# The order of scores, transposed probabilities and turns in the attention stage of a hybrid decoder step

## What is computed

```
qkv, z, b_lg, a_lg, qb, kb, vb, ga, gb = in_proj(hp, norm1_w[l], w_in[l])
q, k, v, g, beta, conv_new = delta_prep(qkv, zeros, b_lg, a_lg, ...)   # causal conv (4 taps) + SiLU, 12 x 128 channels
o_a, s_new = gated_delta_chunked(q, k, v, g, beta, zeros)
y_a = delta_out(o_a, z, delta_norm_w[l], w_proj_a[l])
y_b = moba_prompt(rope(qb), rope(kb), vb) @ w_proj_b[l]                # causal softmax attention, 8 heads of 64
hp = merge_and_mlp(hp, y_a, y_b, ga, gb, w_out[l], ...)                # then squared-ReLU MLP
```

## Time and profile before

| | us |
|---|---|
| three runs | 1039.46, 1040.54, 1044.44 (median 1040.54) |
| the profiled execution | 1039.46 |
| its span in the trace | 1037.3 |
| TensorE busy | 982.2 (95%) |
| VectorE busy | 540.4 (52%) |
| ScalarE busy | 398.5 (38%) |
| GpSimd busy | 235.2 (23%) |

### The profile page before, as it was taken

The page is one execution under the profiler, slowest core; times in us unless marked ns, Lnnn a source line. Parts: engine busy times, 40 slices in busy tenths (PEclk is TensorE's granted clock), DMA queues, the critical chain, the costliest instruction groups (busy, mean ns, idle before and its releaser), DMA issues.

```text
span 1037.3 us, 20446 instructions
## 1 busy us (share of the span) xinstructions
PE 982.2 (95%) x7854; PEld 927.0 (89%) x7854; DVE 540.4 (52%) x727; ACT 398.5 (38%) x673; POOL 235.2 (23%) x137
## 2 busy tenths in 40 slices
PE   5999799999898898999999999998999999999997
PEld 5999788899898676777789999998999999999996
DVE  5246599898678534313314755784344334334443
ACT  6435445555513235332222333342154235224433
POOL 0017666567646301100000000493000000000000
PEclk9999899999978899999999999999999999999998
DMA  8576676667665246777864384235333333233312
GB/s 249 161 239 199 206 227 185 201 176 211 187 179 149 61 127 201 211 211 206 245 176 138 114 263 135 83 102 153 102 92 91 93 91 92 89 93 89 93 41 82
DMA packets 182313, 156.75 MB, mean 151 GB/s; under 512 B 9153, under 2 KB 144011, under 8 KB 181846
## 3 DMA queue, kind: packets, MB, share of 16 engines
q1 hardware_dynamic: 167382, 143.75, 47.2%
q10 hardware_dynamic: 14856, 11.97, 3.6%
HBM read 146.84 MB, written 8.95 MB: 150 GB/s over the span
## 4 chain that ended last, share of the span: by engine, by line
PE 74%; DVE 8%; issue 6%; ACT 4%; POOL 4%; SPq 2%; DMA 1%; ACTq 0%; DVEq 0%; POOLq 0%
PE ps L457 58%; PE ps L2037 5%; PE ps L2028 3%; POOL ring L752 3%; ACT w_high L441 2%; DVE uu L1679 1%; PE ps L1893 1%; DVE w_low L446 1%; SPq L579 1%; DVE lg L1213 1%; DMA ring<-in_cache_v 1%; PE ps L2044 1%; PE ps L1711 1%; SPq L580 1%; PE ps L1860 1%
## 5 line engine op out<-in xcount | busy, mean ns | idle before, releaser
L457 PE MATMUL ps<-xh,w_high 128*128 128x256 f32 x1216 | 258.8, 294 | 7.1 <-DVE cvr L1258 4.3
L446 DVE TENSOR_TENSOR w_low<-w_raw,w_high 128x1024 fp32r<-128x1024 f32 x125 | 165.7, 1325 | 162.8 <-ACT w_high L441 162.3
L457 PE MATMUL ps<-xl,w_high 128*128 128x256 f32 x1216 | 247.3, 285 | 0.0
L457 PE MATMUL ps<-xh,w_low 128*128 128x256 f32 x1216 | 247.0, 285 | 0.0
L441 ACT ACTIVATE w_high<-w_raw 128x1024 fp32r<-128x1024 f32 x125 | 132.2, 1057 | 258.2 <-PE ps L457 255.4
L457 PEld LDWEIGHTS ps<-xh,w_high 128*128 128x128 f32 x1216 | 190.3, 191 | 22.2 <-issue 19.5
L457 PEld LDWEIGHTS ps<-xl,w_high 128*128 128x128 f32 x1216 | 191.2, 191 | 0.0
L457 PEld LDWEIGHTS ps<-xh,w_low 128*128 128x128 f32 x1216 | 190.9, 190 | 0.0
L752 POOL TENSOR_TENSOR ring<-ring,qb 128x1024 f32<-128x1024 f32 x64 | 153.3, 2419 | 140.8 <-DVE mtqk L1228 73.2
L457 PE MATMUL ps<-mh,w_high 128*128 128x256 f32 (+1 forms) x640 | 128.6, 282 | 3.4 <-DVE ml L1669 3.4
L457 PE MATMUL ps<-mh,w_low 128*128 128x256 f32 (+1 forms) x640 | 128.9, 283 | 0.0
(11 more groups left out here) (358 smaller groups left out, 1243.3 us busy)
## 6 DMA issues: line engine op xcount, KB each, us to landing
ring<-in_cache_k SPq DMA_DIRECT2D x128, 256.0 KB, 3.0
ring<-in_cache_v SPq DMA_DIRECT2D x128, 256.0 KB, 3.0
w_raw<-in_w_in SPq DMA_DIRECT2D x66, 256.0 KB, 3.9
w_raw<-in_w_up SPq DMA_DIRECT2D x64, 256.0 KB, 3.0
w_raw<-in_w_down SPq DMA_DIRECT2D x64, 256.0 KB, 3.0
w_raw<-in_w_in ACTq DMA_DIRECT2D x24, 256.0 KB, 4.1
w_raw<-in_w_out SPq DMA_DIRECT2D x16, 256.0 KB, 3.4
ht_dram<-ht ACTq DMA_DIRECT2D x1, 2080.0 KB, 14.1
```

The costliest lines, as they stand in the source:

```text
L446: dve.tensor_tensor(w_low[:, u % 2], w_raw[:, u % 4], w_high[:, u % 2].bitcast(F32), ALU.subtract).then_inc(S_lo, 1)
L457: last = pe.matmul(out[:, a:b], w[:, u % 2, k, :], x[:, i, a:b], start=(first + i == 0 and w is w_high and x is rhs_h), stop=(first + i == ...
```

## The change

It changes the order in which three engines issue the operations of a step, and with it which score is computed in which step.

- PE, step n: before, on odd n two scores (n + 1 and n + 2) in a row, a quarter, `turn_probs(n)`, `pv_prompt(n − 1)`, a quarter, then `turn_conv` and `turn_rows_out`. After, `turn_probs(n)`, the score n + 2 by itself, a quarter, `pv_prompt(n − 1)`, `turn_rows_out`, `turn_conv`, a quarter.
- ACT, step n: before, taps (or tanh), `exp_scores(n + 1)`, `turned_probs(n)`, `conv_turned_out`, `split_high`. After, `turned_probs(n)`, `exp_scores(n + 1)`, taps, `conv_turned_out`, `split_high` on odd n, tanh on even n.
- DVE: `maxima(n + 2)` in step n in place of `maxima(n + 1)`.
- The table of constants gets two more blocks of 128 columns, which nothing reads.

```diff
-K_ID, K_ONE, K_TRI, K_CAUS, K_LT8, K_ROPE = 0, 128, 256, 384, 512, 576
+K_ID, K_ONE, K_TRI, K_CAUS, K_STRICT, K_INCT, K_LT8, K_ROPE = 0, 128, 256, 384, 512, 640, 768, 832
...
             for n in range(NA):
                 q_t, h = divmod(n, HB)
                 m = (n - 1) // 2
+                turned_probs(n)
+                if n + 1 < NA:
+                    exp_scores(n + 1)
                 if n % 2:
                     if m < NC12:
                         conv_taps(m)
                     else:
                         z_tanh(m)
-                elif 2 <= n <= 2 * NC12:
-                    conv_tanh((n - 2) // 2)
-                if n + 1 < NA:
-                    exp_scores(n + 1)
-                turned_probs(n)
-                if n % 2:
                     if 1 <= m <= NC12:
                         conv_turned_out(m - 1)
                     split_high(act, U_C + m + 2)
+                elif 2 <= n <= 2 * NC12:
+                    conv_tanh((n - 2) // 2)
...
+            maxima(1)
             for n in range(NA):
                 q_t, h = divmod(n, HB)
                 m = (n - 1) // 2
-                if n + 1 < NA:
-                    maxima(n + 1)
+                if n + 2 < NA:
+                    maxima(n + 2)
...
             def scores(n):
                 q_t, h = divmod(n, HB)
                 r, N = slice(64 * (h % 2), 64 * (h % 2) + 64), (q_t + 1) * P
+                if n >= 2:
+                    pe.wait_ge(S["att_exp"], n - 1)
+                if n < 2:
+                    pe.wait_ge(S["mt_out"], 11 + n)
+                if n < HB:
+                    pe.wait_ge(S["qk_out"], 5 + n // 2)
                 mm(score_bank(n, N), qt[r, h // 2, q_t * P:(q_t + 1) * P], kt[r, h // 2, 0:N], start=True, stop=True)\
                     .then_inc(S["att_sums"], 1)
-
-            def score_pair(n):
-
-                pe.wait_ge(S["att_exp"], n)
-                if n < HB:
-                    pe.wait_ge(S["qk_out"], 5 + n // 2)
-                scores(n)
-                scores(n + 1)
...
             for n in range(NA):
-                if n % 2 and n + 1 < NA:
-                    score_pair(n + 1)
+                turn_probs(n)
+                if n + 2 < NA:
+                    scores(n + 2)
                 if n + 1 < 2 * NWOVEN:
                     quarter_unit(2 * n + 2)
-                turn_probs(n)
                 if n >= 1:
                     pv_prompt(n - 1)
+                if n % HB == TURN_AT and n >= HB:
+                    turn_rows_out(n // HB - 1)
+                if n % 2 and 3 <= n <= 2 * NC12 + 1:
+                    turn_conv((n - 3) // 2)
                 if n == NA - 1:
                     sum_new_rows()
                 if n + 1 < 2 * NWOVEN:
                     quarter_unit(2 * n + 3)
-                if n % 2 and 3 <= n <= 2 * NC12 + 1:
-                    turn_conv((n - 3) // 2)
-                if n % HB == TURN_AT and n >= HB:
-                    turn_rows_out(n // HB - 1)
```

More of the change, by code:

```diff
@@ L165, in constants @@
     c[:, K_CAUS:K_CAUS + P] = np.where(i[None, :] <= i[:, None], 0.0, -BIG)
+    c[:, K_STRICT:K_STRICT + P] = np.where(i[None, :] < i[:, None], 0.0, -BIG)
+    c[:, K_INCT:K_INCT + P] = np.where(i[:, None] <= i[None, :], 0.0, -BIG)
     n = np.arange(8)
@@ L1910, in _ @@
             quarter_unit(1)
-            pe.wait_ge(S["mt_out"], 11)
-            pe.wait_ge(S["qk_out"], 5)
             scores(0)
@@ L1915, in _ @@
             turn_moba_heads(7)
-            pe.wait_ge(S["mt_out"], 12)
             scores(1)
             for n in range(NA):
-                if n % 2 and n + 1 < NA:
-                    score_pair(n + 1)
+                turn_probs(n)
+                if n + 2 < NA:
+                    scores(n + 2)
                 if n + 1 < 2 * NWOVEN:
                     quarter_unit(2 * n + 2)
-                turn_probs(n)
                 if n >= 1:
                     pv_prompt(n - 1)
+                if n % HB == TURN_AT and n >= HB:
+                    turn_rows_out(n // HB - 1)
+                if n % 2 and 3 <= n <= 2 * NC12 + 1:
+                    turn_conv((n - 3) // 2)
                 if n == NA - 1:
```

## The result

| | before | after |
|---|---|---|
| median (us) | 1041.12 (4 runs) | 1054.46 (4 runs) |
| ratio, 95% interval | | 1.0125, 1.0105 to 1.0144 |
| median of a second set | 1041.18 (23 runs) | 1054.00 (6 runs) |
| ratio of that set | | 1.0120, 1.0102 to 1.0139 |
| profiled execution | 1039.46 | 1052.68 |

The changed kernel is slower by 1.2%, about 13 us. Forecast were a sum of +7.4 us, a time of 1047.5 and a range up to 1053.5: the direction was right, the size too small, and the median lies just outside the range.

A forecast was written before the change was run, and what follows sets the result against it. PE, busy for 95% of the span, was taken as the bound. From the profiled execution, 1039.46 + 11.5 − 4.3 + 1.7 − 1.5 = 1046.9 us, named as 1047.5; the forecast's own range was 1044.5 to 1052.5, the wider one 1042.5 to 1053.5.

The forecast's parts named there:

- The mechanism: PE, attention stage: a pair's heads run side by side, so each score left alone adds a slot; 11.5 us in all.
- the silu's stalls: PE's seven waits for conv_silu before first quarters, 4.3 us, go; new stalls of 1.7 us come, some 1.2 at n = 5.
- DVE's wait for `w_high`: DVE in the attention stage: its 7.1 us wait for w_high was to be gone with the earlier turn_conv.
- the wait for `gate_a`: PE at the end of the stage: the 1.87 us wait hangs on a chain of the same length and stays.
- The walk through the end of the stage: Chain from w_low of step 30 to att_n: att_n starts 7 us later, PE's own work arrives 8.5 later.
- wait for `att_n`: PE at turn_rows_out(3): the 1.48 us wait is absorbed, taken as −1.5 us in the sum.
- 15 slots: Attention stage: 15 single scores each hold PE for a pair's time, 0.43 to 1.06 us, adding 11.5 us.
- the entry of 0.09 us: A single score starts 0.09 us later than the spacing of records before it; paid 15 more times, only in a bound.
- my bound of 12.8: Upper bound on the added PE time of the slots, 12.8 us, with the late start of each single score.
- Faster: Rival: an added slot costs next to nothing and the stalls go, 1033.7 to 1035.4 us; chance 0.06.
- no change: Rival: PE takes the added time out of slack, 1039 to 1043 us; chance 0.14.
- Slower still: Rival: ACT's late taps stall DVE and PE in every pair, 12 times 0.5 us on top, 1053 us; chance 0.10.

The follow-up runs named there:

- experiment 4: Kernel before, pairs kept in a row, but every score reads partitions 0 to 63 of qt and kt: 1046.11 us, ratio 1.0041.
- experiment 2: Kernel before with the second score of each pair moved behind the quarter of a unit that followed the pair: 1054.30 us, ratio 1.0120.
- experiment 7: Changed kernel with ACT's old order, single scores kept: 1052.49 us, ratio 1.0098.
- 11: Kernel before with earlier turns, turn_probs right behind the pair on odd steps, and DVE's silu ahead of the reduces on even steps: 1036.88 us, ratio 0.9959.
- 6: Kernel before with ACT's new order alone: 1069.67 us, ratio 1.0272.
- experiment 1: Changed kernel with the scores in pairs again and maxima(n + 1) in step n, the other moves kept: 1056.38 us, ratio 1.0123.

## Why the prediction came out as it did

**The mechanism was right.** A score alone takes PE as long as a pair, at all widths (0.41 and 1.05 us), because the heads of a pair lie in different partitions (experiment 4). The waits moved as forecast: the silu's stalls went to two, the longest behind the convolution of n = 5 (0.8 us, forecast 1.2), DVE's wait for `w_high` went, one of `conv` for the taps came (1.4 us), the wait for `gate_a` stayed at 1.9. The walk through the end of the stage had its start wrong, though. The chain from `w_low` to `att_n` keeps its 10.3 us, but it starts at 270.28, 11.3 us later than before and not 7, and `gate_a` comes 11.3 later as well. PE arrives 12.3 later and not 8.5. That most of the wait for `att_n` was absorbed all the same came from two errors of like size.

**The step that failed is a term that was sized too small**: "so 15 slots are added: 3 of 0.43, 4 of 0.64, 4 of 0.85, 4 of 1.06, that is 1.3 + 10.2 = 11.5 us". I took the pair's time on PE as the price of a slot, and put the entry of 0.09 us in a bound only. By stretches without a stall a slot costs 1.19 to 1.23 us at 512 keys and 1.00 at 384, which is 0.13 to 0.17 above the values I took, and over all widths it is 0.15 above them (experiment 2). That is 11.5 + 15 · 0.15 = 13.7 us, which also lies above my bound of 12.8. The rise of PE's busy time in the stage, 14.1 us, agrees, where I had named 10. The 0.09 stood in the earlier trace rows. The rest is paid by the instruction behind the score, and the trace of before shows such a cost too: behind a pair the quarter's first two records take 0.35 us from start to start (243.39 to 243.74) where the next two take 0.23. I measured the pair up to the start of the next instruction and not through it.

**The waits, term by term.** The silu: −4.3 + 1.1 against my −4.3 + 1.7. `att_n`: 1.48 down to 0.45, so −1.0 against −1.5. Missed altogether: `turn_probs` at the head of a step waits for `attention_low`, +1.1. The sum as forecast and as the runs give it:

| term | forecast | measured |
|---|---|---|
| 15 slots | +11.5 | +13.7 (14 of them measured) |
| stalls for the silu, old and new | −2.6 | −3.2 |
| `turn_probs` for `attention_low` | none | +1.1 |
| wait for `att_n` | −1.5 | −1.0 |
| sum | +7.4 | +10.6 |
| the stage in the traces | | +10.8, +10.6 |

Of the 5.9 us between +7.4 and the measured 13.3 the slots are thus 2.2, the missed wait 1.1, the other waits −0.1, and 2.7 stand in none of these terms.

**Behind the stage.** The ratio says 13 us, the stage 10.7. The lower ends of the two intervals are at 10.9 and 10.6 us. The time from the wait in the MLP to the end differs by 1.5 us between the two traces of before, by 1.0 between those of after and by 2.5 over all four, the time from the stage to that wait by 2.2 us between the two traces of before (436.0 and 433.8). I had left out such differences, and the first trace had them against the change (2.4 of its 13.2 us: 0.5 ahead of the stage, 1.9 behind it). From the transposes to the end of the span the two traces of before take 767.3 and 766.6 us and those of after 769.2 and 770.0. The traces of the other runs spread from 766.1 to 769.5 us, with 772.6 in experiment 7, whose traced execution was the slowest of its six. Whether some 2 us behind the stage belong to the change stays open. In the other runs the times (by their ratios) and the stages differ as well, with either sign: +4.3 against +4.5 in experiment 4, −4.3 and −4.4 in 11, +28.3 and +29.0 in 6, but +12.5 and +13.6 in 2, +10.2 and +12.3 in 7, +12.8 and +15.7 in 1. In 2 and 7 the shorter wait for `gate_a` (1.0 and 0.8 us in place of 1.9) makes up about 1 us of that. None of them shows a cost behind the stage.

**The rivals.** "Faster" and "no change" fell. "Slower still" gave the right time for a wrong reason: its stalls of DVE in every pair are not there. They are there when the pairs are kept (experiments 1 and 6), and this I hadn't seen: I weighed ACT's late taps in the whole change only. The parts don't add up. Splitting the pairs costs 13 us, ACT's order 28 us, PE's and ACT's moves beside pairs 13 us, and all together 13 us. With a single score in each step DVE can take each maximum a step ahead, and exp no longer waits for it. This line of before is gone from ACT's waits:

```profile
ACT prob L936 <- DVE nbias L1326: 23.6, 18, 2.7
```

ACT's new order then costs next to nothing (experiment 7); but PE pays the slots, and then sets the time by itself. That the maximum a step ahead is what makes ACT's order cheap is argued, since no run moves the maxima alone. With two banks for the scores, a pair and a maximum a step ahead exclude each other in every second step, since the pair fills both.

## What to carry to other kernels

Before an order of matmuls is loosened, look for neighbours that share the array: two products with 64 contraction rows in different halves of the partitions took the time of one, and a quarter of a unit between them ended that. Price an added slot by whole steps of the loop without a stall, or through the instruction behind it, not by the instruction's own time. And a reorder of several queues should be judged as a whole and in parts: here one part cost 28 us alone and nothing that can be told beside the others, and the cheap part, the earlier turns, shortened the stage only once what it ran into was moved as well. Look at the granted clock behind new waits too: in experiment 1 it added half as much again.

## What the runs showed that was not expected

- A product with 64 contraction rows that stands by itself between products of 128 rows costs 0.14 to 0.18 us more than the time it holds PE (1.19 and 1.23 us at 512 keys, for 1.05); 0.09 of it is seen at its start, the rest in the first records behind it.
- Two scores in a row in the same partitions take 1.91 us at 512 keys, less than twice 1.05, and 0.64 at 128, less than twice 0.41: as if a fixed part of some 0.2 us were paid once.
- The same wait of 3.4 us of PE in the same program was followed by a full clock in some executions and by a lowered one in others, worth 1.5 us between two traces of one kernel.
